# Attention's division moved out of attention into retention, and the expert conversions rescheduled

## The reference

```python
x = x + _mixer(_rmsnorm(x, g_norm_mix), ...)
x = x + _hmoe(_rmsnorm(x, g_norm_ffn), ...)

def _dilated_attention(q, k, v):      # 16 heads of 64; (window, dilation) = (128,1), (512,4), (2048,16)
    for window, dilation in DILATED_PATTERNS:
        o, m, d = _dilated_pattern(q, k, v, window, dilation)   # output, row max, denominator
    ...
    num = sum(w * o for w, o in zip(weights, outs))
    return num / sum(weights)          # the division that the change moves
```

## Time and profile before

| what | us |
|---|---|
| three timed runs | 1597.77, 1618.32, 1626.84 (median 1618.32) |
| profiled execution | 1600.68 |
| its span (first to last instruction, core 6, the slowest) | 1596.2 |
| spans of the eight cores | 1581.8 to 1596.2 |
| busy on core 6: TensorE | 1371.4 (86%) |
| VectorE, ScalarE, GpSimd | 765.3, 695.0, 763.7 (48%, 44%, 48%) |

### The profile page before, as it was taken

The page is one execution under the profiler, slowest core; times in us unless marked ns, Lnnn a source line. Parts: engine busy times, 40 slices in busy tenths (PEclk is TensorE's granted clock), DMA queues, the critical chain, the costliest instruction groups (busy, mean ns, idle before and its releaser), DMA issues.

```text
span 1596.2 us, 29866 instructions; the slowest of 8 cores (1581.8 to 1596.2 us)
## 1 busy us (share of the span) xinstructions
PE 1371.4 (86%) x10037; PEld 787.3 (49%) x10037; DVE 765.3 (48%) x1239; ACT 695.0 (44%) x1191; POOL 763.7 (48%) x874
## 2 busy tenths in 40 slices
PE   4889998888879999999999899999999746476575
PEld 2344447777654444444444344444445435355463
DVE  3687774767556656555656411111355662121122
ACT  3576667887753444434443411111233543223232
POOL 1379991332236657666756312221226645354353
PEclk9999998999999999999999899999999867788797
DMA  9747865777865678999984299785964785999985
GB/s 213 212 92 131 166 145 152 175 175 171 176 146 100 112 107 127 127 131 146 125 134 123 55 293 175 119 131 111 261 211 166 212 303 151 265 254 256 261 188 92
DMA packets 105502, 267.03 MB, mean 167 GB/s; under 512 B 43354, under 2 KB 65370, under 8 KB 98818
## 3 DMA queue, kind: packets, MB, share of 16 engines
q0 software_dynamic: 29280, 124.30, 48.6%
q1 hardware_dynamic: 76066, 140.76, 28.2%
HBM read 285.71 MB, written 116.65 MB: 252 GB/s over the span
## 4 chain that ended last, share of the span: by engine, by line
PE 69%; DMA 14%; DVE 4%; issue 4%; ACT 4%; POOL 3%; SPq 1%; POOLq 0%; DVEq 0%; ACTq 0%
PE ps L169 69%; DMA arena<-xn,idx 8%; DMA zret<-arena 5%; ACT arena L169 4%; DVE arena L169 3%; POOL arena L169 3%; DMA arena<-x 1%; DMA cfs_sb<-cfs 1%; SPq L169 1%; DVE arena L167 1%; DMA vp<-arena 0%; ACT L169 0%; DVEq L156 0%; DVE logit L169 0%; POOL wb L169 0%
## 5 line engine op out<-in xcount | busy, mean ns | idle before, releaser
L169 PE MATMUL ps<-arena 128*128 128x512 bf16 (+5 forms) x8208 | 1275.5, 313 | 75.1 <-ACT arena L169 30.2
L169 PEld LDWEIGHTS ps<-arena 128*128 128x128 bf16 (+1 forms) x8208 | 677.4, 102 | 583.4 <-issue 121.5
L169 ACT ACTIVATE arena<-ps 128x512 bf16<-128x512 f32 (+5 forms) x600 | 422.5, 719 | 445.8 <-PE ps L169 416.7
L169 POOL TENSOR_TENSOR arena<-arena 128x512 bf16<-128x512 f32 (+4 forms) x274 | 347.8, 1278 | 296.5 <-DVE arena L169 243.0
L169 DVE TENSOR_TENSOR arena<-ps,arena 128x512 f32<-128x512 f32 (+4 forms) x420 | 235.2, 572 | 337.9 <-PE ps L169 153.5
L169 PE MATMUL ps<-cbs_sb,arena 128*128 128x128 bf16 x1408 | 130.8, 232 | 111.6 <-DMA arena<-xn,idx 76.3
L169 DVE SCALAR_TENSOR_TENSOR arena<-arena,ps 128x512 f32<-128x512 f32 x176 | 115.6, 683 | 192.8 <-PE ps L169 191.3
L169 PEld LDWEIGHTS ps<-cbs_sb,arena 128*128 128x128 bf16 x1408 | 100.3, 104 | 180.8 <-issue 152.0
L169 ACT ACTIVATE arena<-arena 128x8 f32<-128x8 f32 (+5 forms) x225 | 148.6, 665 | 60.1 <-DVE arena L169 24.5
L169 DVE TENSOR_TENSOR arena<-arena 128x1024 bf16<-128x1024 bf16 (+9 forms) x176 | 131.7, 756 | 70.6 <-ACT arena L169 63.6
L169 POOL DMA_INDIRECT out<-arena,idx x48 | 76.3, 1591 | 122.8 <-ACT arena L169 68.8
(11 more groups left out here) (60 smaller groups left out, 340.6 us busy)
## 6 DMA issues: line engine op xcount, KB each, us to landing
wb<-wexp POOLq DMA_DIRECT2D x60, 768.0 KB, 16.0
arena<-wb SPq DMA_DIRECT2D x30, 1536.0 KB, 16.0
arena<-x SPq DMA_DIRECT2D x32, 512.0 KB, 7.2
arena<-vx POOLq DMA_DIRECT2D x12, 768.0 KB, 15.1
arena<-wri POOLq DMA_DIRECT2D x8, 1024.0 KB, 23.2
zret<-arena SPq DMA_DIRECT2D x16, 512.0 KB, 19.0
arena<-zret SPq DMA_DIRECT2D x4, 2048.0 KB, 17.2
out<-arena SPq DMA_DIRECT2D x16, 512.0 KB, 8.2
```

Of the source, the lines that this page charges most:

```text
L169: ins = getattr(engobj, meth)(*a, **kw)
```

## The change

Five things are changed.

1. The division leaves attention. `den_shift`, `den_act` and `z_out` are gone, with their tiles. When a head's four copies are done, SP stores the 64 rows of numerators (512 KB, f32) to a new tensor `num`, and one row of denominators (8 KB) to `den`.
2. In retention the 16 x 2048 denominators are loaded as one tile of 128 x 256, inverted by one VectorE instruction at step 1 and stored to `rden`. From step 4 on each step starts one of 32 units (a pair of heads, 512 positions): `div_load` brings 128 x 512 numerators and twice 512 reciprocals spread over 64 partitions, and five steps later `div_mul` multiplies (VectorE, 128 x 512, f32 to bf16) and stores to `zatt`. There are five buffers of each kind, in the part of the arena that attention's `xo` used.
3. The mask of items n=2 and n=4 is no longer added by matmuls; VectorE multiplies instead. n=3 and n=5 keep `bias`.
4. Conversions go in the order in which the experts are used, in groups of four in that order. 8 are in projection as before, none in attention, 34 in retention (every second step to the end, and steps 0 and 32), 12 in the first merge pass (from its first unit on, three of five units up to un=18), and the last 6 in steps 0 to 5 of the second merge pass.
5. A load of converted weights waits for its group in the new numbering.

```diff
-        CVE = [e for e in range(NE) if e not in EORD[:NDIR]]
-        NCV = 8
-        Rcv = [[] for i in range(NCV)]
+        CVE = EORD[NDIR:]
+        NCV = 4
+        Rcv = [[] for i in range(-(-len(CVE) // NCV))]
...
-        def den_shift(pr, e, hf):
-            r0, d0, i = e * 64, 64 - e * 64, (2 * pr + e) % NXO
-            OP("pool", "tensor_copy", out=den[hf][r0:r0 + 64, :], in_=xo[i][d0:d0 + 64, hf * 1024:(hf + 1) * 1024],
-               reads=Rxo[i][2 * hf:2 * hf + 2], writes=[Rden[hf][e]])
-
-        def den_act(pr, hf, func, scale):
-            OP("act", "activation", out=den[hf], in_=den[hf], func=func, scale=scale, reads=Rden[hf], writes=Rden[hf])
-
-        def z_out(pr, hf):
-            cs = slice(hf * 1024, hf * 1024 + 1024)
-            for e in range(2):
-                r_, i = slice(e * 64, e * 64 + 64), (2 * pr + e) % NXO
-                OP("dve", "tensor_tensor", out=zb[i][r_, cs], in0=xo[i][r_, cs], in1=den[hf][r_, :], op=ALU.mult,
-                   reads=Rxo[i] + [Rden[hf][e]], writes=Rxo[i])
-                if hf == 1:
-                    p.dma(zatt_d[pr * 128 + e * 64:pr * 128 + e * 64 + 64, :], zb[i][r_, :], reads=Rxo[i], writes=[Rzatt[2 * pr + e]],
-                          semkey=("zatt", i))
+        def head_out(pr, e):
+            h, r0, d0, i = 2 * pr + e, e * 64, 64 - e * 64, (2 * pr + e) % NXO
+            p.dma(num_d[h * 64:(h + 1) * 64, :], xo[i][r0:r0 + 64, :], reads=Rxo[i], writes=[Rnum[h]], semkey=("zatt", i))
+            p.dma(den_d[h:h + 1, :], xo[i][d0:d0 + 1, :], reads=Rxo[i], writes=[Rdend[h]], semkey=("xin", i))
...
-                todo.setdefault(g + 1, []).append(lambda: (osb_copy(pr, eh, 3), den_shift(pr, eh, 1)))
-                if eh == 1:
-                    for hf in range(2):
-                        for lag, f in ((1, lambda hf=hf: den_act(pr, hf, AF.Ln, 1.0)), (3, lambda hf=hf: den_act(pr, hf, AF.Exp, -1.0)),
-                                       (5, lambda hf=hf: z_out(pr, hf) if pr < 7 else deferred.append(lambda: z_out(pr, hf)))):
-                            todo.setdefault(g + lag + 4 * hf, []).append(f)
+                todo.setdefault(g + 1, []).append(lambda: (osb_copy(pr, eh, 3), head_out(pr, eh)))
...
-                    if n_ == 9:
-                        convert(1)
...
-            queue.append((pr, eh, n_, S_item(pr, eh, kind, j, n_ in (2, 3, 4, 5))))
+            queue.append((pr, eh, n_, S_item(pr, eh, kind, j, n_ in (3, 5))))
...
+        NDB = 5
+        nb = [alloc([128, 512], F32, [Rnb[i]]) for i in range(NDB)]
+        rb = [alloc([128, 512], F32, Rrb[i]) for i in range(NDB)]
+        zo = [alloc([128, 512], BF16, [Rzo[i]]) for i in range(NDB)]
+        p.dma(dall, den_v, reads=Rdend, writes=[Rdall], semkey="rawtab")
+
+        def den_rec():
+            OP("dve", "reciprocal", out=dall, in_=dall, reads=[Rdall], writes=[Rdall])
+            p.dma(rden_d.rearrange("h (a b) -> (h a) b", a=8), dall, reads=[Rdall], writes=[Rrden], semkey="gqkb")
+
+        def div_load(u):
+            pr, qt, i = u // 4, u % 4, u % NDB
+            cs = slice(qt * 512, qt * 512 + 512)
...
+            for e in range(2):
...
+        def div_mul(u):
+            pr, qt, i = u // 4, u % 4, u % NDB
+            OP("dve", "tensor_tensor", out=zo[i], in0=nb[i], in1=rb[i], op=ALU.mult, reads=[Rnb[i]] + Rrb[i], writes=[Rzo[i]])
...
+        DIV0, NDV = 4, 32
...
-                if deferred:
-                    deferred.pop(0)()
+                if s_ == 1:
+                    den_rec()
+                ud = s_ - DIV0
+                if 0 <= ud - NDB < NDV:
+                    div_mul(ud - NDB)
+                if 0 <= ud < NDV:
+                    div_load(ud)
                 pending = pending[take:]
-                if s_ % 4 != 1 and s_ < 48:
+                if s_ % 2 or s_ % 32 == 0:
                     convert(1)
...
-            if 3 <= un <= 21 and un % 2:
+            if un < 20 and un % 5 in (0, 1, 3):
                 convert(1)
...
+            if s_ < 8:
+                convert(1)
```

More of the change, by code:

```diff
@@ L319, in build_nc @@
     wb_d = nc.dram_tensor("wb", [NE, 128, 6144], BF16, kind="Internal").ap()
+    num_d = nc.dram_tensor("num", [D, S], F32, kind="Internal").ap()
+    den_d = nc.dram_tensor("den", [16, S], F32, kind="Internal").ap()
+    rden_d = nc.dram_tensor("rden", [16, S], F32, kind="Internal").ap()
     zatt_d = nc.dram_tensor("zatt", [D, S], BF16, kind=skind).ap()
@@ L763, in build_nc @@
         xo = [alloc([128, S], F32, Rxo[i]) for i in range(NXO)]
-        zb = [x_.bitcast(BF16)[:, 0:S] for x_ in xo]
-        Rden = [[p.res(f"den{i}_{e}") for e in range(2)] for i in range(2)]
-        den = [alloc([128, S // 2], F32, Rden[i]) for i in range(2)]
-        Rzatt = [p.res(f"zatt{i}") for i in range(16)]
+        Rnum = [p.res(f"num{h}") for h in range(16)]
+        Rdend = [p.res(f"dend{h}") for h in range(16)]
+        Rzatt = [p.res(f"zatt{i}") for i in range(32)]
         slot = [0]
@@ L973, in build_nc @@
             g += 1
-        deferred = []
         for g in sorted(todo):
@@ L1665, in build_nc @@
                 load_wx(q)
-        assert not fill
+        assert not fill and conv_at[0] == 2 * len(CVE)
         route_exp(*pend)
```

21 lines of the change are left out of this document (16 added, 5 removed).

## The result

The changed kernel took 1651.93 us (median of four runs, 1650.04 to 1658.68) where the kernel before, on the same chip, took 1608.69. The ratio is 1.030, 95% interval 1.020 to 1.040: slower. It leaves out the kernel before's longest run, 1626.84, which counts as a slow one, so it is a little more than the quotient of the two medians. The forecast was 1586, with 1556 to 1616 as its range and 0.08 for slower. The profiled execution took 1652.66; core 6 is again the slowest and is compared with the earlier trace rows.

A forecast was written before the change was run, and what follows sets the result against it. TensorE, 98% busy and more in retention and first merge pass, was taken to pace attention's heads too. 1600.7 - 39 - 1 + 4 + 7 + 9 gave 1581, plus 5 for run spread: 1586, range 1556 to 1616.

The forecast's parts named there:

- Attention: Attention stage: without division work and two mask pairs, heads take 10.7 us instead of 13.55; 39 us less (20 to 44).
- What moves into attention's transfers is small: six conversions go: Attention's transfers: six conversions leave, a 512 KB numerator store per head replaces 256 KB; no time counted.
- Rival C: Attention does not follow TensorE, as two score buffers limit it: 12.0 us a head, 18 less gain, 1599; chance 0.10.
- The reciprocal: Retention, once: between nothing and one 886 ns multiplication; with a deferred z_out gone, 1 us less for both.
- the order of conversion: Experts stage: the new order costs nothing, as the last six are needed by the 28th expert at the earliest.
- Quiet, that is nothing: Retention: a step's division loads cost nothing on quiet queues, since a zret store landed in 4.5 us before step 17.
- 40 to 50 us for each of the two bursts, which uses up the lead and a little more: Retention, head-weight backlogs against a 34 us load lead: waits of 2 to 3 us each, 4 us more in all.
- Rival B: Retention steps 17 to 28 and 33 to 40: division starves, two backlogs of 75 us cost 24 each; 1625, chance 0.12.
- fewer conversions: Retention: argument against the division starving; a conversion every second step instead of three in four; no size of its own.
- First merge pass: Conversions at the first two units delay zr(1), wanted by unit 2 with 1.4 us slack: 7 us more (0 to 10).
- Second merge pass: Six conversions in its first steps make x tile 4 land 5 to 11 us late: 9 us more (0 to 20).
- Rival A: Collisions hide: both merge passes cost nothing and retention 2 us; 1563, chance 0.33.

The follow-up runs named there:

- the last kernels: Changed kernel with 16-bit division operands, spread units and third store buffer, 1578.59 us (ratio 0.986); also with seven conversions moved within retention, ratio 0.993.
- conv_pause: Changed kernel with retention's 34 conversions moved out of the division's steps: one in each of steps 0 to 3, none in 4 to 40, rest after; ratio 1.069.
- best3: Kernel with 16-bit division operands, spread units and third store buffer, its seven conversions at head-weight steps moved to steps 10, 14, 24, 26, 28, 30, 46; ratio 0.993.

## Why the prediction was wrong

**Attention: the mechanism right, the size partly by luck.** -36 against -39 - 1. Eight of the 15 gaps between the masks of n=3 are 10.6 to 10.9 us, as forecast:

```profile
255.61 0.32 PE L169 MATMUL ps<-arena,cbs_sb 128*128 128x384 bf16 x1
...
414.82 0.32 PE L169 MATMUL ps<-arena,cbs_sb 128*128 128x384 bf16 x1
```

These are 14 heads in 159.2 us, 11.37 each on the average, where 10.7 was forecast. TensorE waits 1.2 us for ScalarE in the whole stage and not at all for VectorE, so what the division held up is gone; its "issue" waits, 7.5 us, all stayed, where I let half of them go. One term lay hidden: "What moves into attention's transfers is small: six conversions go" was put at nothing and is worth 6 to 13 us, so the share of the division and the masks was sized too high by as much, and that the total fits is luck. Rival C is out by its mechanism, the wait for ScalarE, though 11.37 lies halfway to its 12.0. The reciprocal took 1.7 us, twice my upper bound, and the order of conversion cost the experts nothing (0.8), as said.

**Retention: the step that failed is "Quiet, that is nothing".** I priced the division's loads by their landing in an empty queue and counted packets' turns during the backlog. Neither is the price. A step's 512 KB of reads, in runs of 2 KB, and its stores cost 42% of the engines' time, and this was to be added to the 49% of the conversions and the weights' 18.9 us per head. The share of 0.94 in the earlier trace rows, for 108 us, was in the text as a length of backlog; read as a budget it said that 6% was left there for something new, and 0.66 in the row above it left a third for what takes some 36%. From that, "40 to 50 us for each of the two bursts, which uses up the lead and a little more" could not stand: with 8% free, 18.9 us take over 200 us to work off (an estimate). In place of 2 to 3 us a burst the runs showed 19.1 and 21.0, and the shares explain this size only as far as the sum above goes: how two queues divide full engines, packet for packet in two windows of the last kernels and three to one in one of the changed kernel, stays open.

**Rival B was it, by place and size.** It put the stalls at steps 17 to 28 and 33 to 40 at 48 us in all; they stood there, 40 us of 42. I gave it 0.12. What I held against it ("fewer conversions") was true and not enough: three in four steps cost 89 us beside the division, one in two 42. Its mechanism, loads that fall behind until the lead is used up, was right; its rate was not, so that the size fits is in part luck. The 1.07 packets per engine and us were those of a queue with one store at a time in it; under the same backlog the division, with many loads in flight, got 3321 / (60 x 16) = 3.5, and needed 4.7.

**First merge pass: right place, mis-sized.** zatt and zret for the third unit were late, by 10.9 + 5.2 = 16 us, forecast 7, and the pass lost 19. I counted the conversions of un=0 and 1 alone; the ones that now run to the end of retention are queued ahead of the same loads. With before's places in the merge pass and conversions to the end of retention it still took 222.1 (the kernel with the units spread); with the same places and conversions ended at step 56, 216.3.

**Second merge pass: right place, mis-sized.** The pass lost 24 us, forecast 9. x tile 4 was 27.6 us late, forecast 5 to 11, with 4.5 and 3.9 at its neighbours. The wait at VectorE was read rightly. I had tile 4 land 24 to 30 us after its issue; issued at 1172.2, it landed 47 us later, behind a reload of merge weights and beside five conversions issued from 1151 to 1194.

**Rival A** fell with every one of its terms. The two merge terms together are 43 us against 16, and retention 43.5 against 4: these three add up to 67 of the 75 us by which the span missed; another 4 are attention's, 4 the start and the experts.

## What to carry to other kernels

Before transfers are added to a stretch, add up the shares: how much of the DMA engines' time the stretch already uses, how much the new loads use by themselves (by a row in which such loads run alone, not by the landing time in an empty queue), and how much each burst brings. Here the first two came to 92%, a burst on top was enough for a stall, and a lead of 34 us did not cover it. Background copies are such a load as well: they fit where nothing with little slack is in flight, and moving them is a change of the critical path. And work taken off one engine should go neither to one that slows it nor to a queue that is full.

## What the runs showed of the hardware that was not expected

- A short landing time says little of what loads cost: one 128 x 512 unit per 6.8 us, 512 KB read in runs of 2 KB and 128 KB written, took 42.3% of 16 engines with the `zret` stores in the same queue (6.38 MB from 500 to 560 in conv_pause), while the loads landed in 4.0 us. Beside conversions, runs of 2 KB took 43.2% for 5.81 MB and runs of 4 KB 45.1% for 6.73 (the larger units), so longer runs saved little; half the bytes read, in runs of 1 KB, took 26.9% for 4.74 MB (bf16).
- Beside dense conversions q1 got no more packets than q0, 697 against 700, and with them 7.6% of the engines; a load issued there landed 58.9 us later (best3, from 634 to 671).
- 64 reads of one row of memory cost no more than reads of 64 different rows (retention 426.0 and 430.6).
- Multiplications on GpSimd made VectorE's 128 x 1024 ones, of two inputs, slower by 82% on the average (692 to 1260 ns); those wholly within one of GpSimd's took 1801 ns.
- A TensorE that stands loses its clock too: 0.89 granted in the stage with 24 us of standing, 0.50 where it was idle for 100.
